# Stick-breaking attention: GpSimd adds softplus values over key blocks before they are split, and one pair of later-sum products per unit

## The reference

```
z = einsum('bqhd,bkhd->bhqk', q_block, k[:, :k_end]) * scale
causal = s_pos < t_pos
log_stay = where(causal, -softplus(z), 0.0)
later = cumsum(log_stay, axis=keys, reverse=True) - log_stay
w = where(causal, exp(log_sigmoid(z) + later), 0.0)
o = einsum('bhqk,bkhd->bqhd', w, v)
```

## Time and profile before

| | before |
|---|---|
| median of 3 runs | 1349.67 us |
| the 3 runs | 1350.61, 1349.67, 1349.6 us |
| span of the profiled execution | 1347.6 us |
| PE busy in the span | 1259.4 us, 93% |
| DVE busy | 809.0 us, 60% |
| ACT busy | 548.1 us, 41% |
| POOL busy | 87.6 us, 7% |

### The profile page before, as it was taken

One profiled execution on the slowest core, in us unless ns is written; L12 is line 12 of the kernel. 1 busy time (PEld: TensorE's weight loads), 2 busy tenths in 40 slices (PEclk: granted clock), 3 DMA queues, 4 the chain that ended last, 5 costly groups with the idle time before them and its releaser, 6 DMA issues.

```text
span 1347.6 us, 17323 instructions
## 1 busy us (share of the span) xinstructions
PE 1259.4 (93%) x6143; PEld 1031.7 (77%) x6143; DVE 809.0 (60%) x1246; ACT 548.1 (41%) x886; POOL 87.6 (7%) x108
## 2 busy tenths in 40 slices
PE   5889999879999999999999897878999999999997
PEld 4767777758788888878887675766788888878886
DVE  5856777764677777732267666465577777762222
ACT  5444545444444444431254443324444444441123
POOL 0201222223000000000020000001200000000000
PEclk9989999999999999999999897989999999999997
DMA  7412112103333333322322121211333333323211
GB/s 220 125 32 63 48 48 63 48 4 106 94 94 93 96 103 97 93 94 94 125 63 63 52 74 36 58 32 52 89 95 101 101 93 93 93 94 103 100 62 63
DMA packets 167122, 109.79 MB, mean 81 GB/s; under 512 B 3414, under 2 KB 159390, under 8 KB 167070
## 3 DMA queue, kind: packets, MB, share of 16 engines
q1 hardware_dynamic: 167070, 109.10, 26.9%
HBM read 106.99 MB, written 2.10 MB: 81 GB/s over the span
## 4 chain that ended last, share of the span: by engine, by line
PE 73%; issue 11%; DVE 10%; ACT 3%; POOL 3%; DMA 0%; DVEq 0%; SPq 0%; POOLq 0%; ACTq 0%
PE bank L1500 16%; PE bank L1243 15%; PE bank L1245 14%; PE bank L1244 14%; PE bank L1395 2%; DVE w_lo L813 2%; PE bank L1396 2%; PE bank L1397 2%; PE bank L1513 2%; POOL ar L478 2%; PE bank L1625 1%; POOL ar L490 1%; DVE af L1197 1%; ACT af L581 1%; PE bank L1650 1%
## 5 line engine op out<-in xcount | busy, mean ns | idle before, releaser
L1243 PE MATMUL bank<-y_hi,w_hi 128*128 128x512 f32 x928 | 367.8, 396 | 5.2 <-DVE w_lo L813 2.5
L1245 PE MATMUL bank<-y_hi,w_lo 128*128 128x512 f32 x928 | 363.7, 392 | 0.0
L1244 PE MATMUL bank<-y_lo,w_hi 128*128 128x512 f32 x928 | 363.5, 392 | 0.0
L813 DVE TENSOR_TENSOR w_lo<-raw,w_hi 128x1024 fp32r<-128x1024 f32 x192 | 234.6, 1222 | 180.8 <-ACT w_hi L511 177.6
L511 ACT ACTIVATE w_hi<-raw 128x1024 fp32r<-128x1024 f32 x190 | 200.6, 1056 | 349.5 <-PE bank L1245 159.4
L1243 PEld LDWEIGHTS bank<-y_hi,w_hi 128*128 128x128 f32 x928 | 175.7, 189 | 45.3 <-issue 8.6
L1245 PEld LDWEIGHTS bank<-y_hi,w_lo 128*128 128x128 f32 x928 | 175.5, 189 | 37.2
L1244 PEld LDWEIGHTS bank<-y_lo,w_hi 128*128 128x128 f32 x928 | 175.8, 189 | 36.4 <-issue 1.0
L1500 PE MATMUL bank<-ar,w_hi 128*128 (+1 forms) x640 | 197.3, 389 | 1.6 <-DVE af L1041 1.6
L1500 PEld LDWEIGHTS bank<-ar,w_hi 128*128 128x128 f32 x640 | 120.0, 188 | 27.2 <-DVE af L1041 2.4
L1500 PE MATMUL bank<-ar,w_lo 128*128 (+1 forms) x320 | 124.5, 389 | 0.0
(11 more groups left out here) (181 smaller groups left out, 1461.1 us busy)
## 6 DMA issues: line engine op xcount, KB each, us to landing
raw<-in_a_ffn_up SPq DMA_DIRECT2D x44, 512.0 KB, 3.8
raw<-in_b_ffn_up SPq DMA_DIRECT2D x44, 512.0 KB, 3.8
raw<-in_a_ffn_down SPq DMA_DIRECT2D x22, 512.0 KB, 3.3
raw<-in_b_ffn_down SPq DMA_DIRECT2D x22, 512.0 KB, 3.2
raw<-in_a_w_in SPq DMA_DIRECT2D x20, 512.0 KB, 3.8
raw<-in_w_kv_shared SPq DMA_DIRECT2D x12, 512.0 KB, 3.8
raw<-in_a_w_out SPq DMA_DIRECT2D x8, 512.0 KB, 3.8
raw<-in_b_w_in SPq DMA_DIRECT2D x8, 512.0 KB, 3.9
```

Of the source, the lines that this page charges most:

```text
L813: nc.vector.tensor_tensor(w_lo[:, m % SPLIT, :], raw[:, m % RAW, :], w_hi[:, m % SPLIT, :].bitcast(F32), ALU.subtract).then_inc(lo_done, 1)
L1243: mm(bank, w[0], y[0][:, k, :], start=(k == 0), stop=False)
L1244: mm(bank, w[0], y[1][:, k, :], start=False, stop=False)
L1245: last = mm(bank, w[1], y[0][:, k, :], start=False, stop=(k == KT - 1))
```

## The change

GpSimd adds softplus values over key blocks in float32, before they are split in a high and a low part. In a unit (3, 2) the columns of block 3 are added to the last 128 of the 256 columns of block 2 (one add of 128 columns); in a unit (1,) the last 256 columns get the summed columns of block 2 of the same head (one add of 256 columns). In a unit (0,) nothing is added. So that the values of a unit (3, 2) are still there two units later, they live in sq instead of spf. POOL waits for the add by a semaphore of its own (sp_acc) before it makes the high part.

later_sums then has one pair of matmuls per unit at L1464's place: 128 columns in a unit (3, 2), 256 in a unit (1,), 384 in a unit (0,). Because the unit's own block now holds later blocks too, the triangular product counts them wrongly in the first two kinds of unit; a new matrix nst (-1 where the row is less than the column) takes the place of ones there. The constants grow by 128 columns: the second load has 640 columns instead of 512, and so has the copy to cr.

```diff
-C_NTRI, C_MASK, C_ID, C_NONE, C_D0, C_D1, C_D2, C_E = 0, 128, 256, 384, 512, 768, 896, 1024
-C_ALL = 1536
+C_NST, C_NTRI, C_MASK, C_ID, C_NONE, C_D0, C_D1, C_D2, C_E = 0, 128, 256, 384, 512, 640, 896, 1024, 1152
+C_ALL = 1664
+C_R = 5 * P
...
+    c[:, C_NST:C_NST + P] = -1.0 * (p < q)
...
-        cr = sb("cr", [P, 4 * P], F32R)
+        cr = sb("cr", [P, C_R], F32R)
...
+        def sp_f32(u):
+
+            hp, blocks, n = unit(u)[1:]
+            return (sq if blocks[0] == 3 else spf)[:, hp, 0:n]
...
-            sp.dma_start(cst_nat, cst[:, 0:4 * P]).then_inc(ld_cst, 16)
+            sp.dma_start(cst_nat, cst[:, 0:C_R]).then_inc(ld_cst, 16)
...
-                    nc.gpsimd.tensor_scalar(spb[:, 0, o:o + n], spf[:, u % 2, 0:n], 1.0, 0.0,
-                                            ALU.mult, ALU.add).then_inc(sp_hi, 1)
+                    f = sp_f32(u)
+                    if blocks[0] == 3:
+                        added += 1
+                        nc.gpsimd.tensor_tensor(f[:, 2 * P:3 * P], f[:, 2 * P:3 * P], f[:, 0:P], ALU.add).then_inc(sp_acc, 1)
+                        pool.wait_ge(sp_acc, added)
+                    elif blocks[0] == 1:
+                        added += 1
+                        nc.gpsimd.tensor_tensor(f[:, P:3 * P], f[:, P:3 * P], sp_f32(u - 2)[:, P:3 * P],
+                                                ALU.add).then_inc(sp_acc, 1)
+                        pool.wait_ge(sp_acc, added)
+                    nc.gpsimd.tensor_scalar(spb[:, 0, o:o + n], f, 1.0, 0.0, ALU.mult, ALU.add).then_inc(sp_hi, 1)
...
-                for b in range(3, blocks[-1], -1):
-                    nb = T - P * b
-                    o = sp_at(b, hp)
-                    for s in range(2):
-                        mm(dst[:, n - nb:n], nones_r, spb[:, s, o:o + nb], start=False, stop=False, skip_group_check=True)
+                later = {3: 3, 1: 2, 0: 1}[blocks[0]]
+                nb = T - P * later
+                o = sp_at(later, hp)
+                m = nones_r if blocks[0] == 0 else nst_r
+                for s in range(2):
+                    mm(dst[:, n - nb:n], m, spb[:, s, o:o + nb], start=False, stop=False, skip_group_check=True)
```

More of the change, by code:

```diff
@@ L125, in build @@
         OBS = (banks[6], banks[7])
-        cst_nat = hT[:, 7, :]
+        cst_nat = hT[:, 6:8, :].rearrange("p k t -> p (k t)")[:, 0:C_R]
         ident = cs[:, C_ID - CS_FROM:C_ID - CS_FROM + P]
         nones = cs[:, C_NONE - CS_FROM:C_NONE - CS_FROM + P]
-        ntri_r, mask_r, ident_r, nones_r = (cr[:, c:c + P] for c in (C_NTRI, C_MASK, C_ID, C_NONE))
+        nst_r, ntri_r, mask_r, ident_r, nones_r = (cr[:, c:c + P] for c in (C_NST, C_NTRI, C_MASK, C_ID, C_NONE))
         def gain(norm, k):
@@ L211, in build @@
             "ms_done", "mmx", "mexp", "mpn", "mt_done", "mpt_hi", "mpt_lo", "mav", "mo_hi", "mo_ev"))
-        z_done, z_min, ln_done, sp_max, sp_hi, sp_lo, cum_done, w_exp, wt_hi, wt_lo, av_done, o_hi, o_ev = (sem(n) for n in (
-            "z_done", "z_min", "ln_done", "sp_max", "sp_hi", "sp_lo", "cum_done", "w_exp", "wt_hi", "wt_lo", "av_done",
+        z_done, z_min, ln_done, sp_max, sp_acc, sp_hi, sp_lo, cum_done, w_exp, wt_hi, wt_lo, av_done, o_hi, o_ev = (sem(n) for n in (
+            "z_done", "z_min", "ln_done", "sp_max", "sp_acc", "sp_hi", "sp_lo", "cum_done", "w_exp", "wt_hi", "wt_lo", "av_done",
             "o_hi", "o_ev"))
@@ L469, in _ @@
             squares(0)
+            added = 0
             for t in range(U + 3):
@@ L1004, in _ @@
                         dve.wait_ge(sp_lo, u - 1)
-                    nc.vector.tensor_tensor(spf[:, u % 2, 0:n], banks[2 + u % 4][:, 0:n], ze[:, u % 2, 0:n],
+                    nc.vector.tensor_tensor(sp_f32(u), banks[2 + u % 4][:, 0:n], ze[:, u % 2, 0:n],
                                             ALU.max).then_inc(sp_max, 1)
@@ L1014, in _ @@
                     o = sp_at(blocks[0], hp)
-                    nc.vector.tensor_tensor(spb[:, 1, o:o + n], spf[:, u % 2, 0:n], spb[:, 0, o:o + n].bitcast(F32),
+                    nc.vector.tensor_tensor(spb[:, 1, o:o + n], sp_f32(u), spb[:, 0, o:o + n].bitcast(F32),
                                             ALU.subtract).then_inc(sp_lo, 1)
```

## The result

The changed kernel takes 1366.01 us (median of 4 runs, 1365.41 to 1366.64) against 1349.88 us before (the three runs known from before and one more, 1349.6 to 1350.61): 1.0119 times, with a 95% interval of 1.0107 to 1.0131. It is 16.1 us slower; 16.8 us had been forecast. The profiled span goes from 1347.6 to 1363.6 us.

What follows compares the result with a forecast made beforehand. The prediction took a ring of DVE, ACT and POOL, without PE, to bound the kernel. Adds 15.5, collision 1.5, head 0.3, less 0.5 for removed matmuls, made 16.8 us more: 1366.5 us, range 1358 to 1375.

Steps and rivals of the forecast that it cites:

- What bounds the kernel: First attention: DVE, ACT and POOL waiting on one another set the 30.73 us per head pair, without PE.
- The middle pair's 33.6 us: Sign: a middle head pair's period in the first attention should go from 30.73 to 33.6 us.
- DVE's wait for L490: Sign: DVE's wait for POOL's high part should rise from 0.63 us to 1.14 in most (3, 2) units, 1.41 in (1,).
- The removed matmuls: Later sums on PE: 8.8 us of matmuls go, but only 0.5 us is gained, after DVE's last low part.
- The adds: 24 POOL adds between DVE's max and POOL's high part cost their whole time plus hand-over: 15.5 us.
- The collision: Second (3, 2) unit's slot: POOL's weights copy beside DVE's low part costs 0.29 us, 1.5 us in five pairs.
- The head: Start of the kernel: the larger second load of constants delays the memory's landing by 0.3 us.
- The sum: Whole kernel: 15.5 + 1.5 + 0.3 - 0.5 = 16.8 us slower, giving 1366.5 us.
- the ring: First attention's cycle: DVE's min, ACT's exp and log, DVE's max, POOL's high part, DVE's low part, DVE's next min.
- Rival C: First attention: idle gaps lower PE's clock, late scores and sums add 6 us more: 1372.5 us; chance 0.15.
- Too low if the clock of the pairs' stretch falls below 1: Sign: if PE's clock falls below full speed during the first attention's head pairs, the forecast time is too low.
- PE's idle time should rise by more than 4 us a pair: Sign: in the first attention PE should idle over 4 us more per head pair, waiting on ACT and DVE.

Runs made afterwards that it cites:

- e1: The changed kernel without GpSimd's 24 adds and their waits, so only the matmuls are removed: 1350.48 us, 1.0004 times the kernel before.
- e8: The changed kernel with its 24 adds but all the matmuls of the old later sums put back: 1366.28 us, 1.0120 times the kernel before.
- e3: The changed kernel with the 24 adds on DVE, right after its max, instead of on GpSimd: 1363.07 us, 1.0099 times the kernel before.
- e5: The kernel before with DVE's min of the next unit moved ahead of this unit's low part: 1337.16 us, 0.9909 times the kernel before.
- e6: The changed kernel with DVE's min of the next unit moved ahead of this unit's low part: 1332.36 us, 0.9872 times the kernel before.
- e7: The changed kernel run once more with nothing altered, on one chip with other runs: 1366.79 us, 1.0131 times the kernel before.
- e4: The kernel before with only the constants enlarged, 640 columns instead of 512 in the second load and copy: 1349.79 us, 1.0002 times the kernel before.

## Why the prediction was right, step by step

- **What bounds the kernel.** Shown, by e1 and e8 (matmuls off or on, no change), by e3 (another engine, same place) and by e5 and e6 (other order, 12 and 34 us). The decisive view was that of the waits: DVE busy plus its two waits fill the period, and PE is in neither. The middle pair's 33.6 us were 33.45 and 33.74, and DVE's wait for L490 rose to 1.18 and 1.46 us where 1.14 and 1.41 had been forecast.
- **The removed matmuls.** 0.5 us had been taken, at the end only. The six matmuls before the last triangular product took 0.92 us from start to start; two are left, and these are their rows:

```profile
308.57 0.61 PE L1482 MATMUL bank<-ar,cr 128*128 128x384 f32 x2 [1.49 <-DVE ar L1032]
...
309.03 0.63 PE L1485 MATMUL bank<-ar,cr 128*128 128x512 f32 x2
```

  0.46 us from start to start, so 0.46 gained.
- **The adds.** 15.5 us had been forecast; the durations were right and the hand-over was 0.09 instead of 0.05 us, which makes 16.4.
- **The collision.** Forecast as 0.29 us in five slots, 1.5 us. It came in three of them, and once more where nobody had looked for it, in the last pair's first unit (0.95 us instead of 0.55), some 1.3 us in all. That the sum of the term came out is luck in part. The slot of a second (3, 2) unit without it and one with it, changed kernel:

```profile
189.62 0.56 DVE L1032 TENSOR_TENSOR ar<-sq,ar 128x384 fp32r<-128x384 f32 x1 [1.18 <-POOL ar L508]
...
189.91 0.49 ACT L658 ACTIVATE af<-bank 128x384 f32<-128x384 f32 x1 [1.13 <-PE bank L1485]
...
190.49 0.52 POOL L486 TENSOR_SCALAR ar<-af 128x384 fp32r<-128x384 f32 x1 [0.90 <-ACT af L658]
```

```profile
221.79 0.49 ACT L658 ACTIVATE af<-bank 128x384 f32<-128x384 f32 x1
...
223.02 0.51 POOL L486 TENSOR_SCALAR ar<-af 128x384 fp32r<-128x384 f32 x1
223.09 0.85 DVE L1032 TENSOR_TENSOR ar<-sq,ar 128x384 fp32r<-128x384 f32 x1 [1.19 <-POOL ar L508]
```

  At 189.6 us PE had just run at its lower clock (184.4 to 187.8) and ACT waited 1.13 us for it, which put GpSimd's copy behind DVE's low part. So the step's condition was incomplete: it took PE to be early. The lower clock as the reason is read from the traces and wasn't tried, but for the full pairs they agree. The profiles of the changed kernel and of e7 hold eight such slots in the second to fifth pairs. In four a stretch at the lower clock ends 1.8 to 2.5 us ahead of the low part and there is no collision (the pairs take 33.41 to 33.45 us); in the other four there is none just ahead, and they collide (33.73 and 33.74 us). In the last pair both kernels collide, although in the changed kernel such a stretch ends 1.7 us ahead.
- **The head.** 0.3 us had been taken. e4 can't tell it from nothing; the profiled execution began its attention 0.6 us early.
- **The sum.** +17.4 us from first to last min, -0.5 at the end, -0.6 at the head and -0.4 at the start of the second layer (near 750 us), whose cause wasn't looked for, make the 16.0 us of the spans, but for rounding. The forecast of 16.8 has an error of 0.9 in the hand-overs, set off by the head and by what followed. Both of these are of the size by which single executions differ, so that the sum came within 0.7 us is luck in part; that the adds cost their whole time in the ring is not.
- **Rival C** was half there: PE's clock fell, as it said, after the gaps on PE. PE had been idle for 1.85 us before 149.44 and again before 182.89, each time waiting for DVE. The two stretches at the lower clock that followed in the changed kernel (the clock is the 0.50):

```profile
150.30:153.70 3.40, 3.40 (x10) 2.63 (x9) 3.31 (x6) 1.49 (x3) 0.99 (x1) 0.50 0.07 19
184.40:187.80 3.40, 3.40 (x10) 2.23 (x8) 2.99 (x5) 2.11 (x4) 1.00 (x1) 0.50 0.27 71
```

  But it cost the full pairs no time: pairs with a mean clock of 0.96 and of 0.98 both take 33.45 us, and right after the second stretch the scores are there at 188.81 + 0.44 = 189.25 us and DVE takes them at 190.70, 1.4 us later, without a wait. Two of the prediction's signs failed by this. "Too low if the clock of the pairs' stretch falls below 1": it fell, and the forecast was not too low. "PE's idle time should rise by more than 4 us a pair": it rose from 0.66 to 2.62 us in the first two pairs shown and to 3.49 in the third, since matmuls at the lower clock count as busy for longer. In this case a lower clock on the engine that isn't the bound was no loss.

## What to carry to other kernels

Before giving an idle engine some work, ask between which two instructions it goes. A 7% busy GpSimd had room for 14 us of adds, but not in the one place where everybody waits for it, and there each microsecond added was a microsecond of time. And when an engine at 98% seems to be the bound, look whether anyone waits for it: here one moved instruction of DVE was worth 12 us, and only after it did taking matmuls off PE pay (28.36 against 29.75 us a pair).

## What the runs showed of the hardware

- A GpSimd addition of two float32 operands takes 461 ns at 128 columns, 734 at 256 and 1277 undisturbed at 512: 2.13 ns a column and about 190 ns fixed, a straight line through three sizes. On DVE it takes 292 ns at 128 and 425 at 256.
- A wait of GpSimd on its own last instruction costs 0.09 us (L508 behind the adds, 24 times).
- When GpSimd's high part of the weights and DVE's low part of the softplus overlap, the one that starts later is the longer one. GpSimd first by 0.07 us: DVE takes 0.85 us instead of 0.56 at 384 columns, and 1.09 instead of 0.69 at 512. DVE first by 0.19 us (e1, 512 columns, 175.05 us): DVE takes 0.69 us, and GpSimd 0.98 instead of 0.62. With 0.2 us of overlap left (e1, 165.28 and 165.64 us) they take 0.56 and 0.57 us, and GpSimd alone takes 0.51.
- The time to the first unit of the attention differs by up to 2.3 us between executions in code that is the same but for the size of the constants (114.0 to 116.4 us in eleven profiles), which sets what differences of this kernel can be told apart by one profile.
